# The position bias of the second block's first mixer, added by TensorE

## The reference, cut to what matters

```python
s_loc = einsum(q, k_blk) * scale
s_loc = where(col_valid[:, None, :], s_loc + bias, NEG_INF)
s_ctx = einsum(q, kc) * scale
scores = concatenate([s_loc.reshape(b, h, rows, GRID_W, n_loc), s_ctx], axis=-1)
p = softmax(scores, axis=-1)
o = einsum(p_loc, v_blk) + einsum(p_ctx, vc)      # per head
pool_x = pool_mix(ux, w_pool, pool_scale)         # window means of u, then a product
out_x = concatenate([na_x, pool_x], axis=-1) @ w_out
```

## Time and profile before

| | |
|---|---|
| median of three runs | 2475.0 us |
| the profiled execution | 2480.05 us |
| its span, first to last instruction | 2478.2 us |
| TensorE busy | 2413.4 us, 97% |
| VectorE busy | 1640.6 us, 66% |
| ScalarE busy | 1050.6 us, 42% |
| mean granted TensorE clock | 0.991 |

### The profile page before, as it was taken

One profiled execution on the slowest core, in us unless ns is written; L12 is line 12 of the kernel. 1 busy time (PEld: TensorE's weight loads), 2 busy tenths in 40 slices (PEclk: granted clock), 3 DMA queues, 4 the chain that ended last, 5 costly groups with the idle time before them and its releaser, 6 DMA issues. The chain is left out here.

```text
span 2478.2 us, 30309 instructions
## 1 busy us (share of the span) xinstructions
PE 2413.4 (97%) x12118; PEld 2007.1 (81%) x12118; DVE 1640.6 (66%) x2487; ACT 1050.6 (42%) x1710; POOL 335.7 (14%) x226
## 2 busy tenths in 40 slices
PE   7999999999999999999999989999999999999998
PEld 5888878858888878888888768887888888887987
DVE  7879696474779597534476467756566577586674
ACT  4222235375322225322226375445555544565443
POOL 0234251201244152001020200000000000000000
PEclk9999999999999999999999999999999999999999
DMA  8666453512566363444362616555534465443653
GB/s 286 196 182 209 144 178 93 143 35 68 170 189 209 130 189 102 157 149 153 119 204 77 149 61 186 187 187 170 180 129 159 135 187 188 154 146 111 202 187 130
DMA packets 248140, 386.01 MB, mean 156 GB/s; under 512 B 16384, under 2 KB 155904, under 8 KB 247936
## 3 DMA queue, kind: packets, MB, share of 16 engines
q1 hardware_dynamic: 241824, 372.45, 47.6%
q0 software_dynamic: 6176, 11.64, 2.2%
HBM read 382.83 MB, written 3.11 MB: 156 GB/s over the span
## 5 line engine op out<-in xcount | busy, mean ns | idle before, releaser
L1277 ACT ACTIVATE whi<-raw 128x1024 fp32r<-128x1024 f32 x558 | 562.3, 1050 | 1072.8 <-PE ps L548 688.6
L1907 DVE TENSOR_TENSOR wlo<-raw,whi 128x1024 fp32r<-128x1024 f32 x558 | 689.9, 1276 | 374.9 <-ACT whi L1277 374.3
L546 PE MATMUL ps<-wlo,Hcut 128*128 128x512 f32 (+1 forms) x1888 | 705.7, 374 | 10.4 <-DVE Hcut L2114 3.5
L548 PE MATMUL ps<-whi,Hcut 128*128 128x512 f32 (+1 forms) x1888 | 695.6, 368 | 0.0
L547 PE MATMUL ps<-whi,Hcut 128*128 128x512 f32 (+1 forms) x1888 | 695.2, 368 | 0.0
L546 PEld LDWEIGHTS ps<-wlo,Hcut 128*128 128x128 f32 x1888 | 356.8, 189 | 78.2 <-issue 6.5
L548 PEld LDWEIGHTS ps<-whi,Hcut 128*128 128x128 f32 x1888 | 356.6, 189 | 60.0
L547 PEld LDWEIGHTS ps<-whi,Hcut 128*128 128x128 f32 x1888 | 356.9, 189 | 56.0
L546 PE MATMUL ps<-Hcut,whi 128*128 128x512 f32 (+1 forms) x1032 | 394.3, 382 | 0.0
L547 PE MATMUL ps<-Hcut,wlo 128*128 128x512 f32 (+1 forms) x1032 | 393.8, 382 | 0.0
L548 PE MATMUL ps<-Hcut,whi 128*128 128x512 f32 (+1 forms) x1032 | 393.8, 382 | 0.0
(11 more groups left out here) (269 smaller groups left out, 1815.2 us busy)
## 6 DMA issues: line engine op xcount, KB each, us to landing
raw<-in_w_ffn_gate_up SPq DMA_DIRECT2D x176, 512.0 KB, 4.8
raw<-in_w_mod SPq DMA_DIRECT2D x130, 512.0 KB, 4.4
raw<-in_w_ffn_down SPq DMA_DIRECT2D x88, 512.0 KB, 4.4
raw<-in_ffn_w_in SPq DMA_DIRECT2D x88, 512.0 KB, 4.5
raw<-in_attn_w_in SPq DMA_DIRECT2D x72, 512.0 KB, 4.0
raw<-in_ffn_w_out SPq DMA_DIRECT2D x44, 512.0 KB, 4.2
raw<-in_w_in SPq DMA_DIRECT2D x32, 512.0 KB, 4.6
raw<-in_mlstm_w_in SPq DMA_DIRECT2D x24, 512.0 KB, 4.6
```

Of the source, the lines that this page charges most:

```text
L546: e.matmul(o, L[0], R[1], start=start, stop=False)
L548: return e.matmul(o, L[0], R[0], start=False, stop=stop)
L1277: e.activation(hi_of(n)[:, z], slot(n)[:, z], ACT.Copy).then_inc(*A.up(("hi", n, h)))
L1907: e.tensor_tensor(lo_of(n)[:, z], slot(n)[:, z], hi_of(n)[:, z].bitcast(F32), ALU.subtract).then_inc(*V.up(("lo", n, h)))
```

## The change

For the second layer's mixer only, TensorE adds the bias: after the product of queries and keys it multiplies the unit matrix with the masked bias table of the head (128 x 256 columns, fp32) and accumulates in the same bank. VectorE no longer writes the scores to SBUF: it takes the maximum from PSUM, and ScalarE's exponential reads PSUM and releases the bank. TensorE waits, ahead of each such product, for `masked` of the head pair. The last edit names another event for a wait that only sums after a mixer of `l == 0` use.

```diff
@@ scores of tensor_program
                     w.wait_ge(*A.at(("tt", l, 1, tts[1][-1])))
-                    e.matmul(b[:, 0:512 - k0], QT[p0:p0 + 64, hp, 128 * qt:128 * qt + 128], KT[p0:p0 + 64, hp, k0:512],
-                             start=True, stop=True).then_inc(*T.up(("sc", l, n)))
+                    i = e.matmul(b[:, 0:512 - k0], QT[p0:p0 + 64, hp, 128 * qt:128 * qt + 128],
+                                 KT[p0:p0 + 64, hp, k0:512], start=True, stop=l == 0)
+                    if l:
+                        i0 = 2 if qt == 0 else 0
+                        w.wait_ge(*V.at(("bb", l, hp)))
+                        i = e.matmul(b[:, 0:256].rearrange("p (i c) -> p i c", i=4), ident(), BB[:, h, i0:i0 + 4, :],
+                                     start=False, stop=True)
+                    i.then_inc(*T.up(("sc", l, n)))
                     ring.full(("sc", l, n))
@@ scores of scalar_program
-                    src = SR[n % 6][:, 0:N] if N == 512 else bk(f)[:, 0:N]
+                    copied = N == 512 and l == 0
+                    src = SR[n % 6][:, 0:N] if copied else bk(f)[:, 0:N]
                     i = e.activation(SR[n % 6][:, 0:N], src, ACT.Exp, bias=sm(o + 1), accum_out=sm(o + 2))
-                    if N == 512:
+                    if copied:
                         i.then_inc(*A.up(("ex", l, n)))
                     else:
                         i.then_inc(*A.up(("ex", l, n), ("free", f)))
@@ scores of vector_program
                     src = bk(f)[:, 0:N]
-                    if qt < 2:
+                    if qt < 2 and l == 0:
                         z, i0 = SR[n % 6], 2 if qt == 0 else 0
@@ end of mixer in vector_program
-                sums_user[:] = [(V, ("zs", l, n_items - 1 if l else n_items - 3)), (T, ("px", l, 3))]
+                sums_user[:] = [(T, ("sc", l, n_items - 1)) if l else (V, ("zs", l, n_items - 3)), (T, ("px", l, 3))]
```

## The result

| | before | after |
|---|---|---|
| median, five runs each | 2475.15 us | 2484.66 us |
| the profiled execution | 2480.05 us | 2486.3 us |
| its span | 2478.2 us | 2484.5 us |

The ratio of the runs is 1.0040, with a 95% interval of 1.0029 to 1.0051: **slower by 9.5 us**, of which the interval leaves 7.2 to 12.6. The forecast was 7.2 us and 2482.2; the measured time lies in the upper part of its range, 2476.0 to 2487.0, and the forecast shift at the lower end of the interval.

A forecast was written before the change was run, and what follows sets the result against it. The softmax chain on VectorE and ScalarE bounds the mixer's inner part. TensorE's 48.5 us from 1417.25 end at 1465.8; plus 2.0 clock and 1.1 tail gives 1468.9 against 1461.68: 7.2 us later, 2482.2 us, range 2476.0 to 2487.0.

The forecast's parts named there:

- VectorE and ScalarE set the pace before, TensorE does after: Mixer's inner part: the softmax chain paces it, TensorE idling about 11 us; VectorE loses 13.2 us and stops being the bound.
- The pair: Two heads' scores with bias products on TensorE: no longer side by side, 3.27 us against 1.05, 17.7 us more over eight.
- rival B: TensorE's tile form changes hide: a pair costs 2.56 us, 1.5 us later, 2476.5 us; chance 0.18 with its neighbourhood.
- Rival A: Heads' scores still overlap: a pair costs 1.9 us, 1 to 2 us earlier than before, 2473.5 us; chance 0.10.
- The wait: TensorE in step 0, after the first scores, stands 5.3 us until the masked bias table is there at 1417.2.
- signs of being wrong: Heads' scores starting within 0.1 us, table masked earlier than 1417 us, or TensorE idle over 3 us behind 1418 us.
- The clock: TensorE restarts at 1.2 GHz after the table wait: 4 us of low stretch (1 to 7), costing 2.0 us (0.5 to 3.5).
- The other work: TensorE's remaining mixer work: parts of `u` 5.2 us, transposes 7.0, values 7.5, pooling 3.7.
- The tail: End of the mixer: TensorE's transposes of item 13 and last values wait for ScalarE's copies, 1.1 us (0.5 to 2).

The follow-up runs named there:

- e6: The changed kernel without the bias product and without TensorE's wait for the table; -6.9 us against the kernel before, ratio 0.9974.
- e7: The changed kernel with each bias product issued twice; +16.5 us against the kernel before, ratio 1.0070.
- e1: The changed kernel with both heads' scores issued first, then both bias products; -2.7 us against the kernel before, ratio 0.9987.
- e5: The changed kernel with the scores product over all 128 rows, summing a pair's two heads; +3.4 us against the kernel before, ratio 1.0015.
- e11: The kernel before, VectorE adding the bias, with the bias table's DMAs issued early; -5.8 us against the kernel before, ratio 0.9977.
- e9: The changed kernel with the bias table's DMAs issued ahead of GpSimd's wait for the mixer's input; -0.1 us against the kernel before, ratio 1.0002.
- e8: The changed kernel with both heads' scores before both bias products, eight parts of `u` before step 0, two before step 2; -4.4 us against before, ratio 0.9982.
- e3: The changed kernel with both heads' scores before both bias products and all ten remaining parts of `u` before step 0; -6.0 us against before, ratio 0.9972.
- e2: The changed kernel with all ten remaining parts of `u` ahead of step 0's scores; +0.5 us against the kernel before, ratio 1.0002.
- e10: The changed kernel with both heads' scores before both bias products and the table's DMAs issued early; -7.2 us against the kernel before, ratio 0.9969.

## Why the prediction was right

The sign, the mechanism and most of the size held, the size in part by errors that cancelled. By its own steps:

- *VectorE and ScalarE set the pace before, TensorE does after.* Shown: e6 gains 6.9 us on before by relieving VectorE; e7 loses 7.0 us on the change by 6.9 us of streaming.
- *The pair.* 3.27 us forecast, 3.27 measured. e1 shows the loss of pairing with the form changes as the cause, e5 splits off the form changes: 2.58 us, rival B's number (2.56). Rival A is out: no second head slips past the bias product.
- *The wait.* 5.3 us of standing forecast, 4.44 measured, since the table was masked 4.55 us after the first scores and not 5.4; that moment varies between executions. One of the prediction's own signs of being wrong, a table masked earlier than 1417 us, thereby came true (1413.81; about 1416.4 by the clock of the profile before, whose stage starts 2.6 us later). It took 0.8 us from the wait and left the mechanism as it was.
- *The clock.* This term of the sum was mis-sized. I put the low stretch still ahead at 4 us (1 to 7), 2.0 us of loss. It was 7.4 us (1413.87 to 1421.3), just outside these bounds, and cost 3.4, just inside the 3.5 allowed: four parts of `u` 4.74 us instead of 2.97, the second head's scores 2.00 instead of 1.05, the two bias products 0.52 and 0.12 more.
- *The other work.* Transposes ahead of scores or values took 0.97 us, not 0.87 (1431.12 to 1432.09), and two pooling products 0.54, not 0.44: I had counted a form change only where it enters the bias product. Together 0.5 us.
- *The tail.* 1.1 us forecast, 1.0 measured.

From the first scores to the output product I had 58.0 us; it was 59.4: the wait -0.8, the clock +1.4, the form changes +0.5, 0.3 not assigned. That the shorter wait took back more than half of the clock's error is luck. Against the 50.8 before that is 8.6 us; the medians differ by 9.5, whose interval holds both.

Rival A's sum has a slip: 1417.25 + 37.8 + 2 is 1457.1 and not 1458, so A would have come some 2.6 us earlier than before instead of 1 to 2. It changes nothing here, since A is out.

What I did not see is what the late table cost already. I read VectorE's 9.7 us of waiting as covered by TensorE's work; e11 shows 5.8 us in it, for the kernel before. So of the 8.0 us that an early table gives the change (79.2 to 71.2), 5.8 were no loss of the change. By the stages, the change's own 8.6 us are 6.5 for the unpaired, form-changing bias products, net of VectorE's relief (e9 against e11; the medians say 5.7), and 2.1 for the longer reach of the wait. This is one order of subtracting; the two parts act on each other, and another order would split them otherwise.

## What to carry to other kernels

Before work is put between two matmuls, look whether they run side by side: four records in little more than the time of two are a pair, and a full-array product between them costs the pair and two form changes on top of itself. Put both halves of the pair first, then the rest; here that turned +9.5 us into -2.7, with VectorE's relief in it. And ask of a late input what it costs now, before pricing what a new reader of it will wait.

## What the runs showed of the hardware

- One head's scores alone take as long as two heads' side by side: 1.05 us (1427.85 to 1428.90) against 1.05.
- Changing between 64-row and 128-row products costs about 0.1 us on leaving and 0.1 on entering, at 2.4 GHz: an estimate from the bias products (0.63 and 0.54 against 0.43 us in e5) and from 3.27 against 2.58 us a pair, with four changes in it.
- How long TensorE stood did not settle how long the clock stayed at 1.2 GHz. In the change 4.44 us of standing brought one low stretch of 10.2 us, 7.4 of it behind the wait; in e5 4.96 us brought 6.8; in e7 6.43 us brought 13.7; but in e1 4.84 us brought only 3.4. In e8 2.23 us brought none, in e3 2.31 us brought 3.4. In e2, e9 and e10, where TensorE stood for no more than 1.3 us at a time, the clock stayed at 2.4 GHz through the stage. What made the stretches so different was not tested.
- With the table's DMAs in their old place, masking of the table began 23.2 to 26.3 us after the stage's start from one profiled execution to the next; with the DMAs issued early it began at 15.3 us in all three, and VectorE did not wait for them.
